# RWKV-7 scan on one NeuronCore: steps on the off-diagonal quarters of the array, state and inverse summed in PSUM

## The reference, cut to what matters

```
sa = S @ kk_t
S  = S * w_t - outer(sa, kk_t * a_t) + outer(v_t, k_t)
y_t = S @ r_t
```

## Time and profile before

| | |
|---|---|
| device time, median of 3 runs | 5350.43 us (5349.00, 5350.43, 5361.76) |
| profiled execution, first to last instruction | 5357.0 us, which of the times is its own isn't known; the highest lies 4.8 us above it |
| PE busy | 4962.6 us (93%) |
| DVE busy | 2757.1 us (51%) |
| ACT busy | 1738.7 us (32%) |
| POOL busy | 1341.7 us (25%) |
| mean granted TensorE clock | 0.971 of full speed |

### The profile page before, as it was taken

How to read it: one execution, slowest core, us unless ns; L and a number is a source line. 1 busy time by engine, 2 the same in 40 slices (tenths; PEclk the granted TensorE clock), 3 DMA queues, 4 the chain that set the end, 5 groups by cost and what they waited for, 6 DMA issues and landing times. The chain is left out here.

```text
span 5357.0 us, 121796 instructions
## 1 busy us (share of the span) xinstructions
PE 4962.6 (93%) x47822; PEld 2955.4 (55%) x47822; DVE 2757.1 (51%) x4952; ACT 1738.7 (32%) x4151; POOL 1341.7 (25%) x2817
## 2 busy tenths in 40 slices
PE   5999997999999997899999999969999999999789
PEld 2666663333333333454444444438888888888744
DVE  1334334666666662221222222247777877777576
ACT  1222121443443440232112211224455555555322
POOL 0111111222222220000000000015566565665343
PEclk8999997999999998999999999989999999999999
DMA  7222211000000006442111211136666666666485
GB/s 289 64 63 63 68 60 63 4 23 23 23 23 23 23 5 254 164 139 60 59 59 59 68 63 59 55 91 146 135 148 139 146 148 139 147 147 141 105 269 173
DMA packets 928976, 526.48 MB, mean 98 GB/s; under 512 B 661344, under 2 KB 879072, under 8 KB 921440
## 3 DMA queue, kind: packets, MB, share of 16 engines
q1 hardware_dynamic: 850144, 500.73, 32.5%
q10 hardware_dynamic: 78336, 18.89, 1.7%
HBM read 330.98 MB, written 188.49 MB: 97 GB/s over the span
## 5 line engine op out<-in xcount | busy, mean ns | idle before, releaser
L1565 PE MATMUL p_bU<-keep_hT,p_slab 128*128 128x512 f32 (+1 forms) x2592 | 1029.5, 559 | 12.8 <-DMA p_slab<-in_o_w_in_dram 7.4
L1565 PEld LDWEIGHTS p_bU<-keep_hT,p_slab 128*128 128x128 f32 x2592 | 493.7, 191 | 543.5 <-issue 512.0
L914 PE MATMUL at_bS<-at_qT,at_kT 97*64 97x512 f32 (+1 forms) x2368 | 601.5, 597 | 8.8 <-issue 8.1
L1046 DVE TENSOR_REDUCE at_mx<-at_bM 128x1 f32<-128x512 f32 (+1 forms) x656 | 400.6, 629 | 356.1 <-PE at_bM L880 353.1
L1009 ACT ACTIVATE at_pT<-at_bS 128x512 f32<-128x512 f32 (+1 forms) x592 | 346.8, 591 | 462.6 <-PE at_bS L914 383.9
L1637 DVE SCALAR_TENSOR_TENSOR p_z<-p_u,p_shift,p_z 128x2306 f32<-128x2306 f32 x26 | 68.1, 2621 | 770.2 <-ACT p_z L1595 770.2
L1893 POOL TENSOR_TENSOR rw_g_at<-rw_g_at,rw_g_prod 64x14 f32<-64x14 f32 (+6 forms) x1008 | 340.9, 338 | 79.0
L1891 POOL TENSOR_TENSOR rw_g_prod<-rw_g_at 64x14 f32<-64x14 f32 (+6 forms) x1008 | 334.2, 332 | 79.1
L914 PEld LDWEIGHTS at_bS<-at_qT,at_kT 97*64 97x64 f32 x2368 | 160.6, 137 | 267.4 <-issue 215.3
L837 POOL TENSOR_TENSOR at_sum_pool<-at_sum_pool,at_pT 128x512 f32<-128x512 f32 x128 | 192.8, 1506 | 433.4 <-ACT at_pT L1009 421.9
L933 PE MATMUL at_bO<-at_pT,at_va 128*64 128x512 f32 x1152 | 299.7, 598 | 0.0
(11 more groups left out here) (264 smaller groups left out, 9245.6 us busy)
## 6 DMA issues: line engine op xcount, KB each, us to landing
rw_zin<-scratch_heads SPq DMA_DIRECT2D x144, 512.0 KB, 4.9
rw_XB<-scratch_inverses SPq DMA_DIRECT2D x576, 64.0 KB, 2.6
mod_w<-in_ada_w_dram SPq DMA_DIRECT2D x6, 4096.0 KB, 23.8
scratch_heads<-p_z SPq DMA_DIRECT2D x24, 1024.0 KB, 4.9
rw_lin<-scratch_lora SPq DMA_DIRECT2D x144, 128.0 KB, 5.5
scratch_bv<-rw_bv SPq DMA_DIRECT2D x144, 128.0 KB, 2.2
scratch_products<-rw_NB SPq DMA_DIRECT2D x288, 64.0 KB, 4.3
scratch_y<-rw_ysb ACTq DMA_DIRECT2D x288, 64.0 KB, 2.9
```

The lines of the kernel that those rows point to most:

```text
L914: last = pe.matmul(bS[rows, g % 3, 0:nq * P], kT[:, s, k * P + VH * x:k * P + VH * x + VH], qT[:, s, q0 * P:(q0 + nq) * P], start=True, st ...
L1046: nc.vector.tensor_reduce(mx[:, j, piece:piece + 1], bM[:, (FIRST_ITEM[b] + i) % 2, 0:n], AX.X, ALU.max).then_inc(max_red, 1)
L1565: last = pe.matmul(bU[:, n % 4, 0:w], slab[:, i, k, :], hT[:, k, tok:tok + w], start=(k == 0), stop=(k == KD - 1))
```

## The change

- **Off-diagonal quarters.** A table ACROSS pairs each head's rows with the other half of the partitions. R1, Y, sa's product and far_p now go from one half of the rows to the other half of PSUM. The unturned half of XB is loaded crosswise, so that the series of a head lives on the other half of the partitions, and sa's product reads XT and r1 there and writes back to the head's own half. The update of the state, scores and the series' other products stay on the diagonal. Y moves to bank 2 and the update stays in bank 1 (SU).
- **State carried in PSUM.** `step_begin` adds S to SU by a product with the identity. DVE's carry is one multiplication of SU by the decay for both directions; `decayed` and the tile Sdec go. Carry waits for SU alone (`su_mm`).
- **The series summed in PSUM.** Both directions share bank 7 (SERIES) and bank 6 (PW). `first_order` starts with 16 products of the identity and XB and adds Pm times XB; `higher_orders` adds Pm times X in the same bank. ACT copies SERIES to XT twice (`take_series`); the four additions on DVE go. `blocks` and `take_w` handle both directions at once.
- **Order.** PE splits step_begin into `step_values` (does not need S) and `step_begin`, and interleaves scores, far_p and higher_orders with them. higher_orders moves from the end of body n-1 into the first step of body n, the turn of V behind the first step_begin, the turn of Kc from the first step to the last. ACT's copies of the turned tiles are issued one by one; those of Kt stand at the body's end.
- **DVE to ACT.** The key factors t1 and the two copies of decays (dec) move to ACT, the scaling of a (0.5, 0.5) is folded into constants, so that DVE scales half of ee; the copy of parameters (cur) goes.
- SP's and POOL's orders and instructions are as before, except that four of spread's eight DMAs write to the other half of XB's partitions, and that spread waits for PE's first order instead of DVE's sum.

```diff
 bank = [core.ps(f"bank{i}", [P, 512]) for i in range(8)]
-R1, Y = bank[0], bank[1]
-SA0 = S0 = 2 * C
-XT_AT, X_AT, P_AT = (2, 3), (5, 4), (6, 7)
-TURN_AT = (2, 3, 4)
-SCORES_AT = ((5, 2), (3, 4))
+R1, SU, Y = bank[0], bank[1], bank[2]
+SA0 = 2 * C
+TURN_AT = (4, 4, 3)
+SCORES_AT = ((5, 3), (5, 3))
...

 HEADS2 = [(slice(HP * h, HP * h + HP), slice(C * h, C * h + C)) for h in range(2)]
...
+        def far_p(m, d, chunks):
+
+            for c in chunks:
+                for rows, other in ACROSS:
+                    last = pe.matmul(PW[other, GT * d + C * c:GT * d + C * c + C], NB_[rows, m.kept, d, c, 0, :], XB[rows, m.two, 1, d, c, :],
+                                     start=(d == 0 and c == 0), stop=True, skip_group_check=True)
+            if d == 1 and c == NCH - 1:
+                last.then_inc(p_mm, 1)
+
+        def first_order(m):
+
+            pe.wait_ge(xb_l, 16 * 8 * (m.n + 1))
+            for d in range(2):
+                for c in range(NCH):
+                    for rows, _ in HEADS2:
+                        pe.matmul(SERIES[rows, GT * d + C * c:GT * d + C * c + C], ident[rows, rows], XB[rows, m.two, 0, d, c, :],
+                                  start=(d == 0 and c == 0), stop=False, skip_group_check=True)
+            pe.wait_ge(p_out, m.n + 1)
+            for d in range(2):
+                for c in range(NCH):
+                    for rows, _ in HEADS2:
+                        last = pe.matmul(SERIES[rows, GT * d + C * c:GT * d + C * c + C], Pm[rows, d, c, :], XB[rows, m.two, 0, d, c, :],
+                                         start=False, stop=False, skip_group_check=True)
+            last.then_inc(xt_mm, 1)
+
+        def second_w(m):
+
+            pe.wait_ge(xt_out, 2 * m.n + 1)
+            for d in range(2):
+                for c in range(NCH):
+                    for rows, _ in HEADS2:
+                        last = pe.matmul(PW[rows, GT * d + C * c:GT * d + C * c + C], Pm[rows, d, c, :], XT[rows, m.two, d, c, :],
+                                         start=(d == 0 and c == 0), stop=True, skip_group_check=True)
+            last.then_inc(x_mm, 1)
+
+        def higher_orders(m, d, chunks):
+
+            if d == 0 and chunks[0] == 0:
+                pe.wait_ge(x_out, m.n + 1)
+            for c in chunks:
                 for rows, _ in HEADS2:
-                    last = pe.matmul(bank[P_AT[d]][rows, C * c:C * c + C], NB_[rows, m.kept, d, c, 0, :], XB[rows, m.two, 1, d, c, :],
-                                     start=(c == 0), stop=True, skip_group_check=True)
-            last.then_inc(p_mm[d], 1)
...
-        def higher_orders(m, d):
-
-            pe.wait_ge(x_out[d], m.n + 1)
-            for c in range(NCH):
-                for rows, _ in HEADS2:
-                    last = pe.matmul(bank[XT_AT[d]][rows, C * c:C * c + C], Pm[rows, d, c, :], X[rows, d, c, :],
...
-        def step_begin(n, c):
-
-            pe.wait_ge(s_out, 8 * n.n + 2 * c)
+                    last = pe.matmul(SERIES[rows, GT * d + C * c:GT * d + C * c + C], Pm[rows, d, c, :], X[rows, d, c, :],
+                                     start=False, stop=True, skip_group_check=True)
+            if d == 1 and c == NCH - 1:
+                last.then_inc(xt_mm, 1)
+
+        def step_values(n, c, beside=None):
+
             for d in range(2):
-                u = pos(d, c)
-                for rows, _ in HEADS2:
-                    pe.matmul(R1[rows, C * d:C * d + C], AR[rows, n.six, d, u, 0, :], S[rows, d, :],
+                for rows, other in ACROSS:
+                    pe.matmul(R1[other, C * d:C * d + C], KK_[rows, n.kept, d, pos(d, c), 0, :], Vt[rows, n.kept, d, pos(d, c), :],
                               start=(d == 0), stop=False, skip_group_check=True)
+                if beside:
+                    beside(d)
+
+        def step_begin(n, c, beside=None):
+
+            pe.wait_ge(s_out, 4 * n.n + c)
             for d in range(2):
-                u = pos(d, c)
-                for rows, _ in HEADS2:
-                    last = pe.matmul(R1[rows, C * d:C * d + C], KK_[rows, n.kept, d, u, 0, :], Vt[rows, n.kept, d, u, :],
+                for rows, other in ACROSS:
+                    last = pe.matmul(R1[other, C * d:C * d + C], AR[rows, n.six, d, pos(d, c), 0, :], S[rows, d, :],
                                      start=False, stop=True, skip_group_check=True)
             last.then_inc(r1_mm, 1)
             pe.wait_ge(y_out, 4 * n.n + c)
             for d in range(2):
                 u = pos(d, c)
-                for rows, _ in HEADS2:
-                    pe.matmul(Y[rows, C * d:C * d + C], AR[rows, n.six, d, u, 1, :], S[rows, d, :],
+                for rows, other in ACROSS:
+                    pe.matmul(SU[rows, C * d:C * d + C], Kt[rows, n.kept, d, u, :], Vt[rows, n.kept, d, u, :],
                               start=(d == 0), stop=False, skip_group_check=True)
-            for d in range(2):
-                u = pos(d, c)
-                for rows, _ in HEADS2:
-                    pe.matmul(Y[rows, C * d:C * d + C], KK_[rows, n.kept, d, u, 1, :], Vt[rows, n.kept, d, u, :],
+                    pe.matmul(Y[other, C * d:C * d + C], KK_[rows, n.kept, d, u, 1, :], Vt[rows, n.kept, d, u, :],
+                              start=(d == 0), stop=False, skip_group_check=True)
+                for rows, other in ACROSS:
+                    pe.matmul(SU[rows, C * d:C * d + C], ident[rows, rows], S[rows, d, :],
                               start=False, stop=False, skip_group_check=True)
-                    pe.matmul(Y[rows, S0 + C * d:S0 + C * d + C], Kt[rows, n.kept, d, u, :], Vt[rows, n.kept, d, u, :],
+                    pe.matmul(Y[other, C * d:C * d + C], AR[rows, n.six, d, u, 1, :], S[rows, d, :],
                               start=False, stop=False, skip_group_check=True)
+                if beside:
+                    beside(d)

         def step_sa(n, c):
             pe.wait_ge(r1_out, 4 * n.n + c + 1)
             if c == 0:
-                for d in range(2):
-                    pe.wait_ge(xt_out[d], 2 * n.n + 2)
+                pe.wait_ge(xt_out, 2 * n.n + 2)
             for d in range(2):
-                for rows, _ in HEADS2:
-                    last = pe.matmul(R1[rows, SA0 + C * d:SA0 + C * d + C], XT[rows, n.two, d, pos(d, c), :], r1[rows, d, :],
+                for rows, other in ACROSS:
+                    last = pe.matmul(R1[rows, SA0 + C * d:SA0 + C * d + C], XT[other, n.two, d, pos(d, c), :], r1[other, d, :],
                                      start=False, stop=True, skip_group_check=True)
             last.then_inc(sa_mm, 1)

         def step_end(n, c):
             pe.wait_ge(sa_out, 4 * n.n + c + 1)
             for d in range(2):
-                for rows, _ in HEADS2:
-                    pe.matmul(Y[rows, S0 + C * d:S0 + C * d + C], Bt[rows, n.kept, d, pos(d, c), :], sa[rows, d, :],
-                              start=False, stop=True, skip_group_check=True)
+                for rows, other in ACROSS:
+                    last = pe.matmul(SU[rows, C * d:C * d + C], Bt[rows, n.kept, d, pos(d, c), :], sa[rows, d, :],
+                                     start=False, stop=True, skip_group_check=True)
+            last.then_inc(su_mm, 1)
             for d in range(2):
-                for rows, _ in HEADS2:
-                    last = pe.matmul(Y[rows, C * d:C * d + C], NB_[rows, n.kept, d, pos(d, c), 1, :], sa[rows, d, :],
+                for rows, other in ACROSS:
+                    last = pe.matmul(Y[other, C * d:C * d + C], NB_[rows, n.kept, d, pos(d, c), 1, :], sa[rows, d, :],
                                      start=False, stop=True, skip_group_check=True)
             last.then_inc(s_mm, 1)
...
+        def take_series(m, which):
+
+            a.wait_ge(xt_mm, 2 * m.n + which + 1)
+            if which == 0 and m.since(2):
+                a.wait_ge(s_mm, 4 * (m.n - 2) + 4)
+            nc.scalar.copy(XT[:, m.two].rearrange("p d c t -> p (d c t)"), SERIES[:]).then_inc(xt_out, 1)

...
-        def decayed(n, c):
-
-            v.wait_ge(s_out, 8 * n.n + 2 * c)
+        def carry(n, c):
+
             if c == 0:
                 v.wait_ge(dec_part, 2 * n.n + 2)
                 if n.group == NG - 1:
                     v.wait_ge(dec_last, n.pair + 1)
-            nc.vector.tensor_tensor(sd[:], S[:], dec[:, n.kept, :, c, None].broadcast_to([P, 2, C]), ALU.mult).then_inc(sd_done, 1)
-
-        def carry(n, c):
-
-            v.wait_ge(sd_done, 4 * n.n + c + 1)
-            v.wait_ge(s_mm, 4 * n.n + c + 1)
-            for d in range(2):
-                nc.vector.scalar_tensor_tensor(out=S[:, d, :], in0=Y[:, S0 + C * d:S0 + C * d + C], scalar=dec[:, n.kept, d, c:c + 1],
-                                               in1=sd[:, d, :], op0=ALU.mult, op1=ALU.add).then_inc(s_out, 1)
+            v.wait_ge(su_mm, 4 * n.n + c + 1)
+            nc.vector.tensor_tensor(S[:], SU[:, 0:2 * C].rearrange("p (d v) -> p d v", d=2),
```

(26 more changed lines are left out.)

313 lines of the change are left out of this document (157 added, 156 removed).

## The result

The changed kernel takes 5382.68 us (median of 5 runs, 5374.91 to 5400.77), the kernel before 5360.63 beside it on the same chip (5 runs, 5349.0 to 5363.32). The ratio is 1.0054, 95% interval 1.0036 to 1.0071: **slower by 0.5%**, where 5300 us, faster, was forecast, with 5230 to 5375 as the range. The profiled execution has a span of 5398.8 us.

The account below looks back on a forecast made before the run. Loops through POOL's inversion and SP were taken to bound the scan: 20.09 us a body to 19.4, 0.69 x 72 = 50 us off the profiled 5357.0, giving 5307, or 5300 us as median; range 5230 to 5375.

Parts of the forecast that it names:

- TensorE's own period: PE's time for one scan body: work floor 14.2, plus 0.8 and 1.4 of waits, 16.4 us, bounds 15.5 to 17.5.
- The waits, 0.8 + 1.4: PE, per body: 0.8 us for waits and array shape changes, 1.4 for ACT's order (1.1 at sa's copy, 0.3 at step_sa).
- late by a microsecond: Sign at ACT's copy of sa in step 0: it would come a microsecond late, about 1.1 us lying bare on PE.
- Loops A and B: A: POOL's inversion until the next blocks land, 19.25 us; B: two-body loop through SP and POOL, 19.2 us a body.
- the sign that the prediction itself gave: At PE's far products: the forecast would be wrong in kind if far_p never waits for the spread blocks.
- POOL's inversion, 14.1 us: POOL, first to last operation: 0.5 us off 14.65, between 0 and 1.5, as DVE's work on SBUF operands shrinks.
- DVE under 12: DVE's work per body falls from 15.8 us to below 12 and cannot bind.
- ACT at most 13: ACT's work per body rises from 10.4 us to at most 13, no bound by itself.
- the copy XT between 0.37 and 0.74: Each of ACT's two 512-column series copies takes between 0.37 and 0.74 us.
- Rival 1: PE's array takes records no denser than 0.030 us; body 20.2 to 20.8 us, 5350 to 5400 us; chance 0.16.
- Rival 2: PE's two diagonals do not overlap at 64 columns, added identity products bare; body 21.7 us, 5465 us; chance 0.08.
- Rivals 3 and 4: Rival 3: loops give more, A 18.25, B 18.7, 5245 us, chance 0.15. Rival 4: inversion no loop, 5160 us, chance 0.04.

Follow-up runs that it names:

- e13: Changed kernel plus four stretches of products on constants ahead of the scan; 64 columns on four quarters took 28.0 ns a record, on two quarters 29.3.
- e3: Changed kernel with six of the 14 elimination steps of POOL's inversion left out; 5379.44 us, ratio 1.005 to the kernel before.
- e4: Kernel before the change with six of the 14 elimination steps of POOL's inversion left out; 5339.32 us, ratio 0.997.
- e5: Changed kernel with every product put back on the diagonal quarters, same instructions and operands; 5532.17 us, ratio 1.0334 to the kernel before.
- e7: Kernel before the change with each 128-column scores product split into two of 64, same columns; 5416.16 us, ratio 1.0112.
- e6: Changed kernel with each 128-column scores product split into two of 64, same columns; 5505.62 us, ratio 1.0281 to the kernel before.

## Why the prediction was wrong

- **TensorE's own period, 14.2 + 0.8 + 1.4 = 16.4 us (bounds 15.5 to 17.5): this step failed.** The overlap itself came: the first two R1 products, higher_orders and the rest of step 0 ran from 1.06 to 2.47 us of the body, where on the diagonal alone they take until 3.43. But the 14.2 counted columns in quarters, and the records of four quarters come no faster than their instructions, at 28 ns a record in a long run (e13), not 15. The body took 20.5 us in the median and never under 19.17. The gaps without a wait cost 1.26 us a body, and where a burst runs ahead, the copies between the halves of a step have less time beside it.
- **The waits, 0.8 + 1.4.** Gaps at semaphores went from 0.47 to 3.27 us a body, by 2.8 instead of 1.4. The place was right: ahead of the end of step 0 some 0.95 us, as said ("late by a microsecond"). But the sa product of step 0, behind the turn, starts 1.14 us after the record ahead of it where 0.3 was put (the copy XT stands behind the stores of y, each of which holds ACT for 0.6 us and more), and the end of step 1 has 0.74, which was not counted at all.
- **Loops A and B at 19.25 and 19.2 set the end: wrong in kind**, by the sign that the prediction itself gave: far_p waited for its blocks once in 1300 us. e3 shows no gain from 4 us less of POOL's inversion, e4 0.2 us a body in the kernel before. The earlier trace rows misled: 117.4 us of SP waiting for POOL are 1.8 a body of a queue that is not the bound. And of PE's row ("hardly a gap" in 19.51 us) I had the right reading in hand: TensorE was the bound before, and 64 records more had to be paid unless the overlap covered them.
- **POOL's inversion, 14.1 us:** 14.62 fell to 14.36; half of the half microsecond, in the direction said. It is worth nothing here.
- **DVE under 12, ACT at most 13, the copy XT between 0.37 and 0.74:** 11.1, 12.4 and 0.59.
- **Rival 1** (records no denser than 0.030; period 20.2 to 20.8; 5350 to 5400 us; chance 0.16) is what happened: 20.60 us a body, 5382.68. Its reason was a limit of the array or of issue between two records; in truth bursts go at 14.8 ns, and what holds the body is the supply behind dense stretches together with waits that the rival's sum did not have. That its number was met is luck. The two records within 0.23 us that I held against it show a burst, and a burst proves nothing about a stretch. The rule of the Trainium skill beside it (TensorE: Matmul & The Clock Gate, section on the 56 ns gap: starts never closer than about 25 ns) does not hold across quarters: 14.8 ns in e13. The estimate by it, 18 to 18.6 us, was too low still.
- **Rival 2** (no overlap, 21.7 us a body, 5465): e5 is this case built, 22.46 us and 5532; the sum was 0.8 us short, and the overlap that it doubted is there.
- Rivals 3 and 4 took the loops, or the lack of one, as the question; with TensorE as the bound neither could come.

The 0.4 us a body of the result (0.0054 x 5357/72; 0.5 by the periods) is a balance: the overlap gives 2.1 us (0.028 x 5357/72, e5 against the changed kernel), and the 64 records with the new waits take 2.5, the difference of e5 to the kernel before (0.0334 x 5357/72).

The clock is a term that the forecast put at nothing. From one bonus product to the next, between 3700 and 5000 us, a body of the changed kernel takes 20.76 us as a mean, one of the kernel before 20.16. Where the granted clock stays full it is 20.32 (50 of 62 bodies) and 20.05 (61 of 63), and in e5 22.59 (all 57); in the changed kernel's 12 others it is 22.59. So at full clock the change costs 0.27 us a body, the overlap giving 2.27 and the rest taking 2.54, and 0.33 of the 0.60 goes with the bodies in which the clock fell. These hold the longer pauses too, so that not all of it need be the clock's own price; at most it is half of the time at the lower level, (68.3-22.4)/2/71 = 0.32 us. Why a shortage in one place and a wait in the next combine to just this was not taken apart further. Nor was it tried to merge products of the steps themselves, by laying Kt beside KK for one 128-column load, which would take out more instructions.

## What to carry to other kernels

Count TensorE's instructions as well as its columns: for small products a load and a product cost about 28 ns of supply, however many quarters they spread over, so a use of all four quarters pays if each product carries 128 columns, or if the dense stretches are short; with 64 columns in a long run it gave next to nothing (e13). An identity product that adds an operand to PSUM should be one wide product, not as many as there are blocks. And to find the bound, shorten the suspect in a run by itself: POOL's wait chain and SP's waits looked like a loop that sets the period, and taking 4 us of 14 out of it changed nothing in the changed kernel and 0.2 us a body in the one before. A pause of TensorE can be paid twice, since the clock falls behind some of them.

## What the runs showed that was not expected

- TensorE's instructions arrive at 256 in 3.5 to 3.75 us in e13, where it stands 1.4 to 1.65 us after each 128 records of four quarters.
- The price of a pair of load and product without new columns is 13 ns in the kernel that uses two quarters and 26 ns in the one that uses four (e7, e6); 14 and 22 ns in the bodies at full clock.
- Two waits on a semaphore that already stands cost 79 ns at a product (e13); they add one instruction.
- Records start out of program order where quarters differ. In the changed kernel's timeline of PE second_w (L2013) starts at 4522.33, while step_sa (L2067), all of which precedes it in the program, goes on until 4522.53:

```profile
4522.31 0.27 PE L2067 MATMUL rw_bank<-rw_r,rw_XT 64*64 64x64 f32 x2
4522.33 0.27 PE L2013 MATMUL rw_bank<-rw_XT,rw_Pm 64*64 64x64 f32 x2
...
4522.53 0.23 PE L2067 MATMUL rw_bank<-rw_r,rw_XT 64*64 64x64 f32 x2
```

- The stores of y, issued by ACT, hold it for 0.6 us and more each (median 0.64), and moving them to another place or queue made it worse three times out of three.
